# Gate projections of a two-layer streaming encoder: nine seven-product units per layer in place of six of the eight plain gate tiles

## The chip, the cores and the metric

The kernel runs on one core of a Trainium2 chip. The metric is the device time of one execution in microseconds (us): 2654.01 us, the median of three runs (2653.74 to 2655.6). Five engines work beside each other, each with its own queue: TensorE (PE, and PEld for its weight loads), VectorE (DVE), ScalarE (ACT), GpSimd (POOL) and SyncE (SP), which here only issues DMAs.

## The reference

Two layers over 640 tokens (512 of a prompt, 8 x 16 of samples). The mixer in the middle of each layer is what the change touches:

```python
def _layer(h, ...):
    h = h + 0.5 * _rmsnorm(_swiglu(_rmsnorm(h, g[0]), f1g, f1u, f1d), g[1])
    m, ... = _mixer(_rmsnorm(h, g[2]), ...)
    h = h + _rmsnorm(m, g[3])
    return h + 0.5 * _rmsnorm(_swiglu(_rmsnorm(h, g[4]), f2g, f2u, f2d), g[5])

def _mixer(u, ...):
    proj = u @ w_in            # 1024 -> 1792 (pool, q, k, v, conv) + 3 * 1024 gate logits gl
    ...                        # y_pool (256 wide), y_att (512), y_conv (256)
    gates = sigmoid(gl.reshape(bsz, n, 3, 1024) + b_gate)
    merged = (gates[:, :, 0] * (y_pool @ w_branch[:256])
              + gates[:, :, 1] * (y_att @ w_branch[256:768])
              + gates[:, :, 2] * (y_conv @ w_branch[768:]))
    return merged @ w_out
```

All is float32; inputs and outputs too.

## The kernel before

Activations lie transposed: 128 channels on the partitions, tokens along the free axis in two halves `hf` of 320. Every matrix product is made of three passes of 128x128 weights over 320 columns: weight high x activation high, weight high x activation low, weight low x activation high. A weight tile's high part is a rounded copy (`w_hi`, ACT), its low part the difference (`w_lo`, DVE or POOL). Weights come from HBM into four buffers `raw0` to `raw3`, and are staged from there into four slots of `w_hi` and `w_lo`.

The order is written out by hand: each engine has its own program, and semaphores tie them. Per layer it runs the first feed-forward block, the mixer, and the second feed-forward block. The wide products of the feed-forward blocks are already made in units of seven products instead of eight (`strassen`, lines 755 to 757 hold the matmuls): four input blocks (two halves of the contraction, two token halves) and four weight blocks are combined by sums, so that two output tiles for both token halves need 7 x 4 x 3 = 84 matmuls where the plain way needs 8 x 4 x 3 = 96. In such a unit ACT makes the high parts, DVE the sums of weights and the low part of the first slot, POOL five low parts of 128x512.

The mixer's gates are made the plain way. A loop over the eight output tiles `m` (`pe.Fori(0, KD)`) runs, for one tile, `group`s of 24 matmuls for three gates and two token halves, and the three branch products (2, 4 and 2 tiles of contraction, for both halves): 6 x 24 + 2 x 8 x 3 = 192 matmuls. ACT takes the sigmoid (L1621), DVE scales the sums from PSUM (L2115), multiplies with the branch products and adds (`merge`, L2277 to L2281), and ACT and DVE split the merged tile into `mg_hi` and `mg_lo` (L2291). The weights of two slots at a time are a "pair": ACT L1201, then DVE L1761. POOL has nothing in this loop. SP loads a pair as soon as its `raw` buffers are free; after the loop it stores the rows of the pool and conv state (`pc_out`, L606 and L610), and then loads `w_out`. After the gates 16 groups of 24 matmuls multiply by `w_out`, the columns of which are four pairs.

Of the kernel before, what the change touches and what calls it, by code (L numbers as in the profile page):

```python
# [8 lines left out]
F32R = mybir.dt.float32r  # L9
# [46 lines left out]
MIX_PAIRS = MIX_PROJ + 2 * KD + KD // 2  # L56
MIX_GROUPS = 4 * MIX_PROJ + 12 * KD + 2 * KD
# [7 lines left out]
MIX_RAW = [len([p for p in range(MIX_PAIRS) if p % 2 == s // 2]) for s in range(4)]  # L65
# [30 lines left out]
def trunk_kernel(nc, x_prompt, x_sample, state_pool, state_conv, cache_k, cache_v, norm_g, ffn1_w_gate,  # L96
# [5 lines left out]
    with ctx:  # L102
# [22 lines left out]
        mg_lo = view("mg_lo", 2 * RS * HT, at_r, F32R)  # L125
# [37 lines left out]
        mg_hi = view("mg_hi", KD * NT, at_z, F32R)  # L163
# [9 lines left out]
        w_lo = view("w_lo", 4 * WS, at_w + 16 * WS, F32R)  # L173
        at_w23 = (at_w + 8 * WS, at_w + 24 * WS)
# [49 lines left out]
        prod = sem("prod")  # L224
        snap1, snap2, snap3 = sem("snap1"), sem("snap2"), sem("snap3")
# [104 lines left out]
        def mg_op(part, k, hf):  # L330
            return slot_r(mg_lo, hf, 16 + k) if part else tile(mg_hi, k, hf)
# [45 lines left out]

        def raw_full_mix(s, l, p):
            return 16 * LOADS * (l * LAYER_RAW[s] + FFN_RAW[s] + p + 1)
# [4 lines left out]
        def mix_slot(p, s):  # L384
            return 2 + s if p in (1, MIX_PAIRS - 1) else s

# [90 lines left out]
        def _(sp):  # L477
# [92 lines left out]
            for l in range(DEPTH):  # L570
# [3 lines left out]
                def pair(p, parts, at=None, first=None):  # L574

                    for s in range(2):
                        at_p = p if at is None else at
                        slot = 2 * (p % 2) + s
# [19 lines left out]
                with sp.Fori(0, KD) as m:  # L598
                    pm = m * 2 + MIX_PROJ
                    pair(MIX_PROJ, lambda s, slot: columns(w_in, l, 0, KD, m * P + COL_GATE + D * s, slot), pm)  # L600
                    pair(MIX_PROJ + 1, lambda s, slot: branch_rows(l, m, slot) if s else
                         columns(w_in, l, 0, KD, m * P + COL_GATE + 2 * D, slot), pm + 1)

                sp.wait_ge(pc_made, l + 1)
# [7 lines left out]
                for i in range(KD // 2):  # L612
                    pair(MIX_PROJ + 2 * KD + i, lambda s, slot: columns(w_out, l, 0, KD, (2 * i + s) * P, slot))
                last = w0 + MIX_TILES
                head(1, l, [(w_split, last - 1), (w_split, last), (w_split, last - 3), (w_split, last - 2)])
# [22 lines left out]
        def _(pe):  # L638
# [407 lines left out]

            def mixer(l, seam):
# [76 lines left out]
                with pe.Fori(0, KD) as m:  # L1124
                    pm, gm = m * 2 + MIX_PROJ, g + 4 * MIX_PROJ + 12 * m
                    pair_groups(MIX_PROJ, pm, gm, x_op)
# [11 lines left out]
                po, go = MIX_PROJ + 2 * KD, g + 4 * MIX_PROJ + 12 * KD  # L1138
                for q in range(4):
                    if q % 2 == 0:  # L1140
                        pe.wait_ge(mg_ready, 2 * KD * l + 2 * KD - 1 + q // 2)
                    group(tile_of(po, q % 2), q % 2, go + q, q, mg_op, K8, q // 2)
                pair_groups(po + 1, po + 1, go + 4, mg_op)
                for q in range(8):
# [9 lines left out]
                    group(tile_of(p, c % 2), mix_slot(p, c % 2), go + 8 + q, c, mg_op, K8, q // 4, between)  # L1154
# [36 lines left out]
        def _(act):  # L1191
# [340 lines left out]

            def mixer(l, sm):
                g = l * GROUPS + MIX_GROUP0

                def pair_high(p, s, used, at=None):

                    slot = 2 * (p % 2) + s
                    full = raw_full_mix(slot, l, p // 2 if at is None else at)
                    stage(full, mix_slot(p, s), KD, (group_done, used) if used is not None else None, slot)  # L1540
# [83 lines left out]
                def round_merged(m, hf):  # L1624
                    act.wait_ge(merged, 2 * KD * l + 2 * m + hf + 1)
                    alone(act)
                    copy(at_tile(mg_hi, m, hf), xv[hf][:, :]).then_inc(mg_hi_made, 1)

                def merge_tile(m, last):

                    gm, u = g + 4 * MIX_PROJ + 12 * m, 6 * KD * l + 6 * m
# [988 lines left out]
```

## Time and profile before

| what | us |
|---|---|
| median of 3 runs | 2654.01 |
| the profiled execution, its own time | 2655.74 |
| its span, first to last instruction | 2653.9 |
| PE busy in the span | 2632.4 (99%) |
| DVE busy | 1705.1 (64%) |
| ACT busy | 1073.1 (40%) |
| POOL busy | 901.3 (34%) |

Busy time is the time in which an engine executes something. Matmuls overlap: one lasts 309 ns, but the next starts before it has ended, so a PE that is 99% busy is one whose matmuls follow each other almost without a gap. A line is counted where the instruction is issued, often in a helper. In the views by line a row gives the engine, the operation, what it writes and reads, the count, the busy time with the mean of one, and the idle time of the engine just before. "Clock" is the clock that TensorE was granted, 1.00 for its full level.

### The profile page before, as it was taken

The page shows a single profiled execution, that of the slowest core. Times are in us where ns is not written, and L with a number is a line of the kernel's source. Part 1 is how long each engine was busy: PE and PEld are TensorE (multiplying, and loading weights), DVE is VectorE, ACT ScalarE, POOL GpSimd, SP SyncE. Part 2 cuts the span into 40 slices and gives each one's busy share as a digit, 9 for nine tenths or more (in the row PEclk, how much of TensorE's full clock was granted, in tenths as well). Part 3 has the DMA queues.
Part 4 walks back from the last instruction along what each step waited for, and adds up shares of the span by engine and source line. Part 5 has one row for each costly group of instructions (what it writes and reads, how often), then busy time and mean ns, then how long its engine had stood idle before and what let it go on. Part 6 is the DMA issues. An engine that isn't in the chain of part 4 may idle for free.

```text
span 2653.9 us, 52846 instructions
## 1 busy us (share of the span) xinstructions
PE 2632.4 (99%) x17936; PEld 2592.2 (98%) x17936; DVE 1705.1 (64%) x2592; ACT 1073.1 (40%) x1938; POOL 901.3 (34%) x730
## 2 busy tenths in 40 slices
PE   9999999999999999999999999999999999999998
PEld 8999999989999999999999999998999999999998
DVE  7888824664454888882488886266554457988623
ACT  5444513333333544452344444143333344444412
POOL 4655203140001565530256651043100035666112
PEclk9999999999999999999999999999999999999999
DMA  4232323212222222323222232231222222322321
GB/s 131 72 93 81 88 77 90 85 48 73 78 74 82 62 73 81 92 75 87 84 72 80 79 94 85 69 109 54 65 71 71 81 79 58 87 79 87 88 73 62
DMA packets 431022, 210.44 MB, mean 79 GB/s; under 512 B 44777, under 2 KB 429259, under 8 KB 430859
## 3 DMA queue, kind: packets, MB, share of 16 engines
q1 hardware_dynamic: 427252, 205.17, 27.0%
q10 hardware_dynamic: 3638, 3.51, 0.4%
q8 instruction: 84, 1.38, 0.2%
q14 instruction: 48, 0.39, 0.0%
HBM read 205.12 MB, written 5.29 MB: 79 GB/s over the span
## 4 chain that ended last, share of the span: by engine, by line
PE 92%; DVE 6%; ACT 1%; issue 1%; POOL 1%; DVEq 0%; ACTq 0%; POOLq 0%
PE ps L755 11%; PE ps L757 11%; PE ps L756 11%; PE ps L661 9%; PE ps L663 9%; PE ps L662 9%; PE ps L860 7%; PE ps L861 7%; PE ps L862 7%; PE ps L691 5%; PE ps L743 4%; DVE mid_lo L2022 2%; PE ps L1010 1%; PE ps L988 1%; PE ps L891 1%
## 5 line engine op out<-in xcount | busy, mean ns | idle before, releaser
L2447 POOL TENSOR_TENSOR w_lo<-raw,w_hi 128x512 fp32r<-128x512 f32 x288 | 426.5, 1491 | 362.9 <-ACT w_hi L1193 361.2
L755 PE MATMUL ps<-x_r,w_hi 128*128 128x320 f32 x1728 | 534.2, 309 | 0.0
L757 PE MATMUL ps<-x_r,w_lo 128*128 128x320 f32 x1728 | 534.0, 309 | 0.0
L1761 DVE TENSOR_TENSOR w_lo<-raw,w_hi 128x1024 fp32r<-128x1024 f32 (+1 forms) x236 | 289.8, 1232 | 340.7 <-ACT w_hi L1201 340.6
L2398 POOL TENSOR_TENSOR acc_y<-acc_y,sq 128x320 f32<-128x320 f32 x95 | 95.3, 1003 | 1086.8 <-ACT sq L1211 1083.4
L756 PE MATMUL ps<-x_r,w_hi 128*128 128x320 f32 x1440 | 445.0, 309 | 0.0
L1201 ACT ACTIVATE w_hi<-raw 128x1024 fp32r<-128x1024 f32 (+1 forms) x244 | 248.9, 1026 | 470.7 <-PE ps L862 293.9
L860 PE MATMUL ps<-mid_hi,w_hi 128*128 128x320 f32 x1392 | 433.6, 311 | 5.1 <-DVE mid_lo L2022 4.5
L861 PE MATMUL ps<-mid_lo,w_hi 128*128 128x320 f32 x1392 | 430.2, 309 | 0.0
L862 PE MATMUL ps<-mid_hi,w_lo 128*128 128x320 f32 x1392 | 430.1, 309 | 0.0
L661 PE MATMUL ps<-x_r,w_hi 128*128 128x320 f32 x1088 | 345.3, 317 | 0.0
L663 PE MATMUL ps<-x_r,w_lo 128*128 128x320 f32 x1088 | 336.1, 309 | 0.0
L662 PE MATMUL ps<-x_r,w_hi 128*128 128x320 f32 x1088 | 336.0, 309 | 0.0
L1193 ACT ACTIVATE w_hi<-raw 128x512 fp32r<-128x512 f32 (+1 forms) x360 | 255.8, 713 | 176.9 <-DVE raw L1891 87.8
L755 PEld LDWEIGHTS ps<-x_r,w_hi 128*128 128x128 f32 x1728 | 324.4, 188 | 0.8 <-issue 0.8
L757 PEld LDWEIGHTS ps<-x_r,w_lo 128*128 128x128 f32 x1728 | 324.4, 188 | 0.0
L756 PEld LDWEIGHTS ps<-x_r,w_hi 128*128 128x128 f32 x1440 | 270.3, 188 | 0.0
L860 PEld LDWEIGHTS ps<-mid_hi,w_hi 128*128 128x128 f32 x1392 | 261.4, 188 | 7.6 <-DVE mid_lo L2022 7.2
L861 PEld LDWEIGHTS ps<-mid_lo,w_hi 128*128 128x128 f32 x1392 | 261.4, 188 | 0.3
L862 PEld LDWEIGHTS ps<-mid_hi,w_lo 128*128 128x128 f32 x1392 | 261.3, 188 | 0.0
L661 PEld LDWEIGHTS ps<-x_r,w_hi 128*128 128x128 f32 x1088 | 204.2, 188 | 11.2 <-issue 6.2
L662 PEld LDWEIGHTS ps<-x_r,w_hi 128*128 128x128 f32 x1088 | 204.5, 188 | 0.2
(235 smaller groups left out, 5093.0 us busy)
## 6 DMA issues: line engine op xcount, KB each, us to landing
raw<-in_ffn_w_gate_dram SPq DMA_DIRECT2D x352, 128.0 KB, 2.3
raw<-in_ffn_w_up_dram SPq DMA_DIRECT2D x352, 128.0 KB, 2.3
raw<-in_ffn_w_down_dram SPq DMA_DIRECT2D x348, 128.0 KB, 2.2
raw<-in_w_in_dram SPq DMA_DIRECT2D x304, 128.0 KB, 2.3
raw<-in_w_branch_dram SPq DMA_DIRECT2D x64, 128.0 KB, 2.6
raw<-in_w_out_dram SPq DMA_DIRECT2D x64, 128.0 KB, 2.3
raw<-in_ffn_w_down_dram SPq DMA_DIRECT2D x68, 64.0 KB, 1.9
rows<-in_x_prompt_dram SPq DMA_DIRECT2D x4, 512.0 KB, 6.0
```

Of the source, the lines that this page charges most:

```text
L661: pe.matmul(bank(b), wh, op(0, k, hf), start=k == ks[0], stop=False)
L662: pe.matmul(bank(b), wh, op(1, k, hf), start=False, stop=False)
L663: mm = pe.matmul(bank(b), wl, op(0, k, hf), start=False, stop=k == ks[-1])
L755: pe.matmul(bank(b), wh, lhs(0, k), start=begin and k == 0, stop=False, skip_group_check=True)
L756: pe.matmul(bank(b), wh, lhs(1, k), start=False, stop=False, skip_group_check=True)
L757: mm = pe.matmul(bank(b), wl, lhs(0, k), start=False, stop=k == QK - 1, skip_group_check=True)
L860: pe.matmul(bank(b), wh, mid_op(0, k, hf), start=first and k == a, stop=False, skip_group_check=True)
L861: pe.matmul(bank(b), wh, mid_op(1, k, hf), start=False, stop=False, skip_group_check=True)
L862: mm = pe.matmul(bank(b), wl, mid_op(0, k, hf), start=False, stop=last and k == z - 1, skip_group_check=True)
L1193: return act.activation(dst, src, ACT.Copy)
L1761: dve.tensor_tensor(w_cols(1, hi_slot, 0, nk), raw_cols(raw_slot, 0, nk), f32(w_cols(0, hi_slot, 0, nk)), ALU.subtract).then_inc(w_split, 1)
L2447: pool.tensor_tensor(w_cols(1, slot, k0, k0 + QK), src, f32(w_cols(0, slot, k0, k0 + QK)), ALU.subtract).then_inc(ws_lo, 1)
```

## The change

Of the eight output tiles two (`PLAIN_M = 2`) stay as they were; their loop is written out. The other six are made in nine units per layer (`GATE_U = 9`): three pairs of tiles, each for the three branches b = u mod 3. A unit has the seven products P1, P2, P6, P5, P7, P4, P3 of 12 matmuls. The branch products of a unit's two tiles (s = 0 and 1) run in the following unit, the first behind P2 and the second behind P7. Their weights come by DMAs of their own into `br_raw`, which lies in `w_lo` slot 3, so that the low part is made in place. Of the four combinations of activations that the units need, three are made during the two plain tiles (`block_sums`), the fourth (`difference_high`) at the first unit. POOL makes five low parts of 128x512 per unit. The merged tiles are held in `mg` and two other buffers, and split into the slots of `x_r` in the last unit. The first pair of `w_out` takes slots 0 and 1 during the last unit, the second pair slots 2 and 3 behind the last branch product (before: slots 0 and 1 for both, the last pair alone in 2 and 3). The stores of `pc_out` come before the units, and ACT and DVE wait for their end. The diff, cut to its core:

```diff
+PLAIN_M = 2
+GATE_U = 3 * (KD - PLAIN_M) // 2
+BRANCH_K = ((0, 2), (2, 6), (6, 8))
+BRANCH_BANKS = (4, 6, 7)
+        br_raw = view("br_raw", QK * P, at_w + 16 * WS + 4 * (3 * WS + QK * P))
         def mix_slot(p, s):
-            return 2 + s if p in (1, MIX_PAIRS - 1) else s
+            return 2 + s if p in (1, PLAIN_PAIRS + 1, MIX_PAIRS - 1) else s
...
@@ SP @@
+                def gate_unit(u):
+                    for s in range(2):
+                        slot = 2 * ((PLAIN_PAIRS + u) % 2) + s
+                        free = (w_split, w0 + 2 * (PLAIN_PAIRS + u) + s - 3) if u < 2 else (gu_lo, low_gate("B22", l, u - 2))
+                        load(slot, columns(w_in, l, 0, KD, COL_GATE + D * (u % 3) + P * gate_tile(u, s), slot), free)
+                def branch(u, s):
+                    b = u % 3
+                    if u == 0:
+                        sp.wait_ge(gu_prod, prod_gate("P1", l, 0))
+                    elif b == 0:
+                        sp.wait_ge(br_done, 2 * branch_no(l, u - 1, s))
+                    else:
+                        sp.wait_ge(br_done, 2 * (branch_no(l, u, 0) if (b, s) == (1, 1) else branch_no(l, u - 1, 1)))
...
+                for u in range(2):
+                    gate_unit(u)
                 sp.wait_ge(pc_made, l + 1)
...
+                for u in range(GATE_U):
+                    if u + 2 < GATE_U:
+                        gate_unit(u + 2)
+                    else:
+                        out_pair(u + 2 - GATE_U, [(gu_lo, low_gate("B22", l, u))] * 2)
+                    for s in range(2):
+                        branch(u, s)
...
@@ PE @@
+                for u in range(GATE_U):
+                    at, a, d = GATE_U * l + u, BANK_A[u % 2], BANK_D[u % 2]
+                    first = u == 0
+                    pe.wait_ge(gu_w0_lo, at + 1)
...
+                    product("P1", u, lambda part, k: x_op(part, k, 0), a, True)
+                    if not first:
+                        pe.wait_ge(gu_c11_out, at)
+                    product("P2", u, lambda part, k: x_op(part, QK + k, 0), BANK_E, True)
+                    if not first:
+                        branch(u - 1, 0)
+                    pe.wait_ge(gu_lo, low_gate("T2", l, u))
+                    pe.wait_ge(gu_snap1, at + 1)
+                    product("P6", u, lambda part, k: s_op(1, part, k), a, False, made(1) if first else None)
+                    pe.wait_ge(gu_lo, low_gate("T1", l, u))
...
+                    product("P5", u, lambda part, k: s_op(0, part, k), d, True, made(0) if first else None)
+                    pe.wait_ge(gu_lo, low_gate("T3", l, u))
+                    pe.wait_ge(gu_snap2, at + 1)
+                    product("P7", u, lambda part, k: x_op(part, k, 1), a, False, s3_made if first else None)
+                    if not first:
+                        branch(u - 1, 1)
+                    pe.wait_ge(gu_lo, low_gate("T4", l, u))
+                    pe.wait_ge(gu_snap3, at + 1)
+                    product("P4", u, lambda part, k: x_op(part, QK + k, 1), a, False)
+                    pe.wait_ge(gu_lo, low_gate("B22", l, u))
+                    pe.wait_ge(gu_c22_out, at + 1)
+                    product("P3", u, lambda part, k: s_op(2, part, k), d, False, made(2) if first else None)
+                for s in range(2):
+                    branch(GATE_U - 1, s)
-                with pe.Fori(0, KD) as m:
+                for m in range(PLAIN_M):
...
@@ ACT, gates() @@
+                    if first:
+                        for k in range(QK):
+                            difference_high(k)
+                        for what in ("T3", "T4"):
+                            t_high(what, 0, None)
+                        b22_high(0)
+                        snap(u, "P6", u2[u % 2][:, :], a, None, gu_snap2)
...
+                    if final:
+                        merged_high(range(0, 6))
+                    else:
+                        t_high("T2", u + 1, "P6")
+                        t_high("T1", u + 1, "P5")
+                    if u:
+                        branch_high(u - 1, 1)
...
+                act.wait_ge(pc_stored, 16 * PC_STORES * (l + 1))
+                gates(l, g + 4 * MIX_PROJ + 12 * PLAIN_M, difference_high, pair_high)
...
@@ DVE, gates() @@
+                    else:
+                        gate_w0_low(l, u + 1)
+                        gate_sums_second(l, u + 1)
+                    if u:
+                        merges(u - 1, 0)
+                    if final:
+                        merged_low(range(2, 6))
+                    if u:
+                        branch_low(u - 1, 1)
...
@@ DVE, plain tiles @@
+                    block_sums(2 * m)
                     gate(4, u, gm + 4, 0)
-                    merge(0, gm + 5, u + 7)
-                    merged_low(m, 0)
+                    block_sums(2 * m + 1)
+                    merge(m, 0, gm + 5, u + 7)
```

On ACT the loop over tiles alternates sigmoids with the two pairs. One turn of it had, in its second part (`mg_hi` is the merged tile's high part, `xv` the merged tile):

```order
L1193 ISA [waits merged]
L1193 ACTIVATE mg_hi<-xv_122 128x320
L1201 ACTIVATE w_hi<-raw_126 128x1024 [waits group_done,raw_loaded2]
L1619 REGISTER_ALU
L1621 ACTIVATE sig_110<-scaled_112,prm 128x320 [waits evac]
L1200 REGISTER_ALU [waits raw_loaded3]
L1201 ACTIVATE w_hi<-raw_127 128x1024 [waits group_done]
```

Now ACT has this in the third unit (u = 2), from the copy of P1 (`s_0_52<-ps`) to the copy of P7 (`u_56<-ps`); `br_raw` holds the branch weights of the unit before, and `gu_prod` counts the products:

```order
L1385 ACTIVATE s_0_52<-ps 128x320 [waits gu_c11_out,gu_prod]
L1385 ACTIVATE w_hi<-raw_124 128x1024 [waits gu_prod,raw_loaded0]
L1768 ACTIVATE sq_131<-sq_131,prm 128x320 [waits gu_scaled]
L1385 ACTIVATE u_0_54<-ps 128x320 [waits gu_c12_out,gu_prod]
L1385 ACTIVATE w_hi<-raw_124 128x512 [waits gu_prod,gu_t_made]
L1385 ACTIVATE w_hi<-t_one 128x512 [waits gu_prod,gu_t_made]
L1385 ACTIVATE w_hi<-br_raw 128x512 [waits br_in1]
L1385 ACTIVATE u_56<-ps 128x320 [waits gu_c22_out,gu_prod]
```

The high part of the second branch tile stands behind the high part of `t_one` (T1), which waits for P5.

On DVE the same unit has, from the low part of slot 0 to the read of C22 (`tb` are the terms to be added into `mg`):

```order
L2503 TENSOR_TENSOR w_lo<-raw_124,w_hi 128x1024 [waits gu_w0_hi]
L2523 TENSOR_TENSOR raw_124<-t_one,raw_125 128x512 [waits gu_t_made,gu_w0_lo]
L2525 TENSOR_TENSOR raw_124<-raw_124 128x512 [waits gu_t_made]
L2575 TENSOR_TENSOR tb_141<-ps,sq_132 128x320 [waits br_done,merged,gu_sig]
L2575 TENSOR_TENSOR tb_142<-ps,acc_x_137 128x320 [waits br_done]
L2565 TENSOR_TENSOR mg<-mg,tb_141 128x320 [waits br_out]
L2565 TENSOR_TENSOR mg<-mg,tb_142 128x320 [waits br_out]
L2546 TENSOR_TENSOR w_lo<-br_raw,w_hi 128x512 [waits br_hi_made]
L2620 TENSOR_TENSOR diag_133<-ps,u_56 128x320 [waits gu_snap3]
```

The loop before had the scaling, the multiplications and additions with the pairs' low parts between them:

```order
L2277 TENSOR_TENSOR xv_122<-ps,sig_105 128x320 [waits sig_done]
L2274 REGISTER_ALU
L2279 TENSOR_TENSOR tb_142<-ps,sig_107 128x320 [waits group_done]
L2280 REGISTER_ALU
L2281 TENSOR_TENSOR xv_122<-xv_122,tb_142 128x320 [waits evac]
```

The low part of the second branch tile now stands behind four instructions of the merge.

On SP the stores of `pc_out` stood behind the last turn of the loop; now they stand behind the loads of the second unit:

```order
L557 DMA raw_127<-in_w_in_dram 128x2x128 [waits w_split]
...
L557 DMA raw_125<-in_w_in_dram 128x2x128 [waits w_split]
L557 DMA raw_125<-in_w_in_dram 128x2x128 x3
L704 DMA out_dram<-pc_out 15x256 [waits pc_made]
L704 DMA out_dram<-pc_out 2x256
...
L557 DMA raw_126<-in_w_in_dram 128x2x128 [waits gu_lo]
```

The last row is the load of the third unit, behind all stores.

## Rows read from the trace of the kernel before

**Rows 1.** Table by time, columns in its first row: gate loop, then feed-forward units.
```profile
core 0: us, PE busy (x) PEld busy (x) DVE busy (x) ACT busy (x) POOL busy (x), PEclk, DMA share, GB/s
596.50:821.80 225.30, 225.30 (x1538) 225.30 (x1537) 108.95 (x182) 77.79 (x108) 0.00 (x0) 1.00 0.26 74
...
96.00:318.00 222.00, 220.83 (x1504) 220.30 (x1503) 198.38 (x286) 114.23 (x226) 119.03 (x81) 1.00 0.31 87
```

**Rows 2.** The chain that ended last, 600 to 866 us; then whom PE waited for longest.
```profile
by line: PE ps L663 33.4%; PE ps L662 33.4%; PE ps L661 33.3%
...
PE ps L860 <- DVE mid_lo L2022: 4.5, 4, 1.1
```

**Rows 3.** PE by line: count, busy us, mean ns, idle before.
```profile
L755 PE MATMUL ps<-x_r,w_hi 128*128 128x320 f32 x1728 | 534.2, 309 | 0.0
...
L661 PE MATMUL ps<-br_hi,w_hi 128*128 128x320 f32 x256 | 79.1, 309 | 0.0
```

**Rows 4.** ACT by line and shape, same columns.
```profile
L1193 ACT ACTIVATE w_hi<-raw 128x512 fp32r<-128x512 f32 x288 | 179.5, 626 | 125.5 <-DVE raw L1891 87.8 <-PE ps L743 19.9 <-PE ps L757 17.0
L1193 ACT ACTIVATE w_hi<-raw 128x1024 fp32r<-128x1024 f32 x72 | 76.4, 1061 | 51.4 <-PE ps L757 44.7 <-PE ps L743 6.6
...
L1193 ACT ACTIVATE u<-ps 128x320 f32<-128x320 f32 x148 | 64.6, 437 | 260.1 <-PE ps L757 259.2
...
L1193 ACT ACTIVATE br_hi<-ps 128x256 fp32r<-128x256 f32 x20 | 7.7, 385 | 22.0 <-PE ps L1038 13.9 <-PE ps L1043 8.1
```

**Rows 5.** DVE by line and shape.
```profile
L1761 DVE TENSOR_TENSOR w_lo<-raw,w_hi 128x1024 fp32r<-128x1024 f32 x172 | 219.6, 1277 | 143.3 <-ACT w_hi L1201 143.1
L1872 DVE TENSOR_TENSOR w_lo<-raw,w_hi 128x1024 fp32r<-128x1024 f32 x72 | 141.6, 1967 | 33.7 <-ACT w_hi L1193 33.5
...
L1905 DVE TENSOR_TENSOR up<-up,inv_x 128x320 f32<-128x320 f32 x108 | 79.2, 734 | 5.9 <-DVE up L1902 1.2
...
L1882 DVE TENSOR_TENSOR t_one<-raw,raw 128x512 f32<-128x512 f32 x72 | 51.7, 718 | 0.0
...
L2115 DVE TENSOR_TENSOR scaled<-ps,inv_x 128x320 f32<-128x320 f32 x96 | 47.2, 492 | 160.4 <-PE ps L663 160.4
...
L2281 DVE TENSOR_TENSOR xv<-xv,tb 128x320 f32<-128x320 f32 x64 | 31.5, 492 | 2.2
...
L2162 DVE TENSOR_TENSOR br_lo<-ps,br_hi 128x256 fp32r<-128x256 f32 x16 | 6.7, 417 | 6.8 <-ACT br_hi L1193 6.8
```

**Rows 6.** DVE in order of time, a low part made beside POOL in a feed-forward unit.
```profile
205.18 2.32 DVE L1872 TENSOR_TENSOR w_lo<-raw,w_hi 128x1024 fp32r<-128x1024 f32 x1
```

**Rows 7.** POOL by line and shape.
```profile
L2447 POOL TENSOR_TENSOR w_lo<-raw,w_hi 128x512 fp32r<-128x512 f32 x288 | 426.5, 1491 | 362.9 <-ACT w_hi L1193 361.2 <-POOL acc_x L2403 1.4
```

**Rows 8.** DMA issues: count, size of one, median us from issue to landing.
```profile
raw<-in_w_in_dram SPq DMA_DIRECT2D x304, 128.0 KB, 2.3
raw<-in_w_branch_dram SPq DMA_DIRECT2D x64, 128.0 KB, 2.6
...
out_dram<-kv_out SPq DMA_DIRECT2D x32, 8.0 KB, 1.4
```

**Rows 9.** Instructions in order of time on ACT, then DVE, second plain tile: start, us.
```profile
638.97 1.06 ACT L1201 ACTIVATE w_hi<-raw 128x1024 fp32r<-128x1024 f32 x1 [2.01 <-PE ps L663]
...
640.07 1.22 DVE L1761 TENSOR_TENSOR w_lo<-raw,w_hi 128x1024 fp32r<-128x1024 f32 x1 [0.51 <-ACT w_hi L1201]
```

**Rows 10.** SP in order of time, around the second and the last gate tile.
```profile
641.52 2.67 SPq L489 DMA_DIRECT2D raw<-in_w_branch_dram  x4
...
786.00 5.28 SPq L610 DMA_DIRECT2D out_dram<-pc_out  x16
```

**Rows 11.** PE in order of time where its clock fell, and the table by time there.
```profile
908.28 0.41 PE L691 MATMUL ps<-x_r,w_hi 128*128 128x320 f32 x1 [0.53 <-DVE x_r L1779]
909.36 2.81 PE L691 MATMUL ps<-x_r,w_hi 128*128 128x320 f32 x11 [0.66 <-DVE x_r L1779]
...
911.40:914.80 3.40, 3.40 (x13) 3.01 (x12) 2.84 (x5) 3.37 (x5) 0.00 (x0) 0.50 0.11 31
```

More of the change, by code:

```diff
@@ L604, in _, with out_pair @@
+                def out_pair(i, first=None):
+                    pair(PLAIN_PAIRS + i, lambda s, slot: columns(w_out, l, 0, KD, (2 * i + s) * P, slot), first=first)
+                for u in range(2):
+                    gate_unit(u)
                 sp.wait_ge(pc_made, l + 1)
@@ L611, in _ @@
                                       pc_out[DEC_T * (b + 1) - nr:DEC_T * (b + 1), c:c + 2 * P]).then_inc(pc_stored, 16)
-                for i in range(KD // 2):
-                    pair(MIX_PROJ + 2 * KD + i, lambda s, slot: columns(w_out, l, 0, KD, (2 * i + s) * P, slot))
+                for u in range(GATE_U):
[5 more added lines that the diff above has]
+                        branch(u, s)
+                for i in range(2, KD // 2):
+                    out_pair(i)
                 last = w0 + MIX_TILES
-                head(1, l, [(w_split, last - 1), (w_split, last), (w_split, last - 3), (w_split, last - 2)])
+                head(1, l, [(w_split, last - 3), (w_split, last - 2), (w_split, last - 1), (w_split, last)])
                 ffn(1, l)
@@ L1629, in merge_tile, with sums_high @@
-                def merge_tile(m, last):
-                    gm, u = g + 4 * MIX_PROJ + 12 * m, 6 * KD * l + 6 * m
+                    act.activation(x_op(0, k, 1), (acc_x + acc_y)[k][:, :], ACT.Copy, scale=gcol(l, 2, k)).then_inc(gs3_hi, 1)
+                def sums_high(k):
+                    at = QK * l + k
+                    if k:
+                        act.wait_ge(gs_made, 3 * at - 2)
+                    act.activation(sq[0][:, :], tile(h, QK + k, 1), ACT.Copy, scale=gcol(l, 2, QK + k)).then_inc(gs_a22, 1)
+                    for j in range(3):
+                        act.wait_ge(gs_made, 3 * at + j + 1)
+                        copy(s_op(j, 0, k), (sq[1], diag[0], diag[1])[j][:, :]).then_inc(gs_hi, 1)
@@ L1643, in merge_tile @@
[L1643 to L1646 removed]
+                    if m + 1 < PLAIN_M:
+                        pair_high(p + 2, 1, gm + 12)
                 act.wait_ge(kv_stored, 16 * KV_STORES * (l + 1))
                 alone(act)
[L1649 removed]
+                for m in range(PLAIN_M):
+                    merge_tile(m)
+                act.wait_ge(pc_stored, 16 * PC_STORES * (l + 1))
@@ L2331, in mixer @@
                 a = (sm + 1, y_mix, l, 3)
-                pair_low(po + 3, 0)
-                take(0)
-                pair_low(po + 3, 1)
-                for q in range(1, 4):
+                for q in range(4):
                     take(q)
```

462 lines of the change are left out of this document (401 added, 61 removed).

## The prediction, made before the changed kernel ran

> **What bounds the kernel now.** I read the table by time first, over the stretch that the change rewrites: the gate loop of the first layer. In its 225.30 us PE is busy for all 225.30, the clock is at 1.00 (2.4 GHz), DVE is busy for 108.95, ACT for 77.79 and POOL for nothing [rows 1]. The loop issues 8 x 192 = 1536 matmuls, so one costs 225.30 / 1536 = 0.1467 us; its 309 ns [rows 3] are mostly overlap. Next the chain of waits: from 600 to 866 us it consists of the three matmul lines alone, a third each [rows 2]. The view of who waited for whom agrees: PE's longest total anywhere is 4.5 us, in the down projections, and the gate matmuls have no idle time before them [rows 2, 3]. So PE's matmul count sets the time here, nothing is hidden behind another engine, and a matmul less is worth 0.1467 us in full, as long as what feeds PE keeps up. Units of the kind that the change brings exist already in the feed-forward blocks. There DVE is busy for 198.38 of 222.00 us (89%) and POOL for 119.03, and PE still for 220.83 [rows 1], with no idle before L755 [rows 3]. So such units can run without a gap, but with little room on DVE.
>
> **What goes.** A unit makes in 84 matmuls what took 96. Nine units in two layers: 18 x 12 = 216 matmuls, 216 x 0.1467 = 31.7 us. The branch products keep their count (192 per layer), and so does `w_out`. The removed work of DVE and ACT was beside PE: worth nothing. The sums of activations in the two plain tiles are 12 DVE and 16 ACT instructions of about half a us in 56 us in which DVE is half idle, with POOL wholly free for their low parts: nothing.
>
> **Timetable of a unit.** A product is 12 x 0.1467 = 1.76 us. From a matmul's start to the next is 0.147, its end comes 0.16 later, and a waiting engine starts 0.04 after its releaser has ended (ACT ends at 638.97 + 1.06 = 640.03, DVE starts at 640.07 [rows 9]): I take 0.2 us from the end of a product to its reader's start. A unit with the branch products of the one before has 108 matmuls (15.8 us), or 132 (19.4 us) where these are the attention branch's. DVE per unit: 1.97 (low of slot 0, beside POOL) + 4 x 0.72 (sums) + 4 x 0.49 (PSUM reads) + 3 x 0.73 (scaling) + 0.8 to 1.4 (branch lows) + 4 x 0.49 (products with the branches) + up to 4 x 0.49 to 0.73 (additions) [rows 5] = 12 to 15 us. POOL: 5 x 1.49 = 7.5 us [rows 7]. Mean use of DVE is about that of the feed-forward units, so throughput is not the limit; order is. Most things have a unit's length to be ready. Four places don't:
>
> 1. Second branch tile, behind P7. Let e be the end of the first tile's product. P6, P5, P7 give 5.28 us. ACT makes its high part only behind T1's, which waits for P5: e + 3.52 + 0.2 + 0.63 (T1 [rows 4]) = e + 4.35. With two contraction tiles: + 0.39 (ACT, 256 columns [rows 4]) + 0.42 (DVE [rows 5]) = e + 5.16, just in time if nothing stretches it; T1's and T2's low parts run on POOL at that moment, and beside POOL the DVE's 1024-column low part takes 1.97 on average where it takes 1.28 otherwise [rows 5], once 2.32 [rows 6]. Bounds 0 and 1.0 late; I take 0.3, since most stretched ones grow by half: five units per layer, 1.5 us.
> 2. The same with four contraction tiles. Its load waits for the first tile's product (one buffer): e + 0.2, two issues of 0.67 (2.67 / 4 [rows 10]), landing 2.6 after the second's start [rows 8] = e + 3.5, before ACT comes to it. Then e + 4.35 + 0.63 + 0.72 = e + 5.70: 0.4 late, up to 1.4 when stretched; I take 0.7. Units 2 and 5: 1.4 us. In the last unit six high parts of the merged tiles (0.44 each and more) stand ahead in place of T2 and T1, from e + 2.4 to about e + 5.1; then 0.63 + 0.72: e + 6.4, 1.1 us late.
> 3. The last unit's first branch tile: its load waits for the second product of unit 7, and P4 and P3 give 3.52 us: 0.2 + 2.6 + 0.39 + 0.42 = 3.6, with the hand-overs 0.3 us late.
> 4. Entry. P1 is due at 596.5 + 2 x 28.16 = 652.8. ACT's first high part waits for the stores of `pc_out` to end. SP comes to them when the second unit's loads are issued, where the second load row ends now: 641.52 + 2.67 = 644.2, or 0.6 earlier; 18 issues of 5.28 / 16 = 0.33 us end at about 650.1 [rows 10], and 1.4 us (stores of `kv_out` [rows 8]) later the last has landed: 651.5. Then 1.06 (ACT) and 1.28 (DVE): P1 at 653.9, 1.1 us late; without the stores it would be 0.2, with a slower landing 2. What is queued behind ACT's wait are the units' high parts; behind DVE's are the sums and the merge of the last plain tile, whose banks P5 needs only 5 us later. P6 then needs T2's low part: three sums on DVE to 655.9, ACT to 656.6, POOL behind T1's low part 656.9 to 658.4, due at 657.4: 1.0 late (bounds 0.5 and 1.5). The first unit has no branch between P7 and P4, so P4 waits for ACT's copy of P7: 0.2 + 0.44 + 0.05 = 0.7. Entry: 2.8 us.
>
> Sum per layer: 1.5 + 1.4 + 1.1 + 0.3 + 2.8 = 7.1 us; two layers 14.2. Net 31.7 - 14.2 = 17.5 us.
>
> Costed at nothing: the loads of the next units (8 issues from 2.5 us into a unit, landed by 9, read 5 us or more later; behind a held-up branch load they land by 14 and are read at 22); POOL's low parts (a unit of time each); `w_out`'s pairs. The first pair's low parts are made in the last unit. The second pair waits for the last branch product and is due 72 + 24 matmuls (14 us) later, with about 7 us of work on ACT and DVE ahead of it. If that cover were gone it would cost the 1.06 + 1.28 of one slot. The last merged tiles (k = 6, 7) are read 10.6 us behind the branch products and need about 6. The way from the mixer into the next block keeps its instructions.
>
> **A rule against the change.** On what the low parts cost beside POOL the rows give growth by half on average, 0.69 on 1.28 [rows 5]. The Trainium skill (SBUF — State Buffer, Who interferes with whom) says that a DVE instruction with two SBUF inputs and a GpSimd instruction that reads SBUF hold the shared read interface in turn, whichever issues second being fully blocked until the first ends. The trace agrees in kind: PSUM-reading L2115 stays at 492 ns, and the 2.32 us one has 1.04 more than the mean alone. By the mean growth the sum is the one above; by a full block at each place it is the second rival.
>
> **The rivals.** *Everything covered*: the feed-forward units carry as much and have no gap [rows 1, 3]; against it stand the entry's fixed chain and place 2. With only 1.5 us left per layer, net 28.7: 2627 in the profiled execution, 2625 as a median; with less than that 2622.
>
> *A full block at each branch tile*: the second tile's low part has to wait for the whole of T1's low part on POOL (1.49 us [rows 7]): 5.16 + 1.49 - 5.28 = 1.4 late in five units, 0.4 + 1.49 = 1.9 in two. 7.0 + 3.8 + 1.1 + 0.3 + 2.8 = 15.0 per layer, net gain 1.7: 2652, no change.
>
> *Slower: the clock falls at these stalls.* At 908 to 910 us two waits of 0.53 and 0.66 us for DVE come close together, and then from 911.40 to 914.80 the clock stands at 0.50 (1.2 GHz), and 13 matmuls start in 3.40 us, which at 0.1467 each would be 1.9 [rows 11]: 1.5 us lost. If the blocked branch tiles brought this in eight units of a layer, that would be 15.0 + 12.0 = 27.0 per layer, 54 - 31.7 = 22 us slower: 2677 (2675 as a median). It decides from a mean of 31.7 / 18 = 1.8 us lost per unit. Against it: PE also waited in the down projections, up to 1.1 us at once [rows 2], and the clock table of the whole stretch 96 to 318 stays at 1.00 [rows 1]; and these waits would be 16 us apart, one at a time.
>
> That fewer matmuls are issued but each costs more is not plausible, since both kinds of group show 309 ns without idle [rows 3].
>
> **How the numbers follow.** The profiled execution before took 2655.74 us, its span 2653.9, and the median is 1.7 below it. 2655.74 - 17.5 = 2638.2; as a median 2636.5. Chances: forecast 0.55 (its own range 2628 to 2647), everything covered 0.26, full block 0.13, slower 0.06. 0.2% is 5.3 us and about what a measurement tells here. Faster by more: 0.55 + 0.26 + half of the block case, less a little for the forecast's tail: 0.86. Within: 0.07; slower: 0.07. The range for 8 in 10 reaches from the covered case to just short of the block case: 2622 to 2650.
>
> **What would show it.** PE's count falls by 216 to 17720. PE idle stands before the first matmul of P6, P4 and P1 in the first unit, and before L1177 (first matmul of a branch tile) behind P7, released by DVE's L2546; little stands before all other products. L2546 has two durations, short where POOL is idle. The clock in the gate stretch stays 1.00. I am wrong on the size of the stalls if PE waits elsewhere, above all before P1 or P3 of units 1 to 7 (DVE behind altogether), or if the matmul pitch in the units is not 0.147 us; and on the entry if ACT doesn't wait for the stores.

## The result and the profile after

| | median of 4 runs, us | lowest to highest | span of the profiled run |
|---|---|---|---|
| before | 2653.88 | 2653.3 to 2655.6 | 2653.9 |
| after | 2668.07 | 2666.92 to 2668.7 | 2666.5 |

The ratio is 1.0052 (95% interval 1.004 to 1.0064): the changed kernel is 14 us slower, where 17.5 us faster was forecast. The forecast was wrong in its sign, and the result lies outside its range of 2622 to 2650.

First the page after, its first lines and the chain:

```profile
span 2666.5 us, 51480 instructions
...
PE 2611.7 (98%) x17720; PEld 2564.3 (96%) x17720; DVE 1823.4 (68%) x2756; ACT 1130.4 (42%) x2114; POOL 1057.7 (40%) x860
...
PE 87%; DVE 9%; ACT 2%; issue 2%; POOL 1%; DMA 0%; DVEq 0%; SPq 0%; ACTq 0%; POOLq 0%
```

PE's count is the forecast one, and still PE holds only 87% of the chain (92% before). Next whom PE waited for (total us, times, longest), the answer to the waits of [rows 2]:

```profile
PE ps L1177 <- DVE w_lo L2546: 16.0, 16, 2.1
PE ps L1161 <- ACT u L1385: 9.8, 2, 4.9
PE ps L965 <- DVE mid_lo L2346: 4.9, 7, 1.1
...
PE ps L1177 <- DVE tb L2575: 2.4, 2, 1.4
...
PE ps L1161 <- DVE w_lo L2503: 1.9, 2, 1.0
PE ps L1161 <- POOL w_lo L2987: 1.7, 2, 0.9
...
PE ps L1161 <- DVE x_r L2589: 1.4, 2, 0.7
```

All but the third are new. L1177 is the first matmul of a branch product, L1161 that of a unit's own products. The same by time, from the last matmul that reads `wp_now`, among the last projections, to the first of the layer's next sum (it reads `ones`): first and second layer after, then before. Columns as in [rows 1].

```profile
592.37:872.94 280.57, 263.77 (x1758) 259.81 (x1756) 183.47 (x287) 120.36 (x217) 88.21 (x73) 0.99 0.27 76
1904.94:2185.82 280.88, 264.43 (x1757) 260.49 (x1755) 183.44 (x287) 120.33 (x217) 88.15 (x73) 0.98 0.27 76
```
```profile
592.75:866.37 273.62, 273.62 (x1865) 273.32 (x1864) 126.40 (x205) 91.67 (x129) 13.60 (x12) 1.00 0.27 78
```

Before, PE is busy for all of it; after, it is idle for 16.80 and 16.45 us, and the clock is below 1.00. The account, from the starts of PE's matmuls:

- Before, the stretch has 1864 matmuls and took 273.62 us, 0.17 above 1864 x 0.1467.
- After, it has 1756 and took 280.57 and 280.88 us, which is 22.96 and 23.28 above 1756 x 0.1467. So a layer saved 108 x 0.1467 = 15.84 us and lost 23.1.
- Between the two stretches it is 1032.00 us in both kernels. From the second to the last matmul it is 473.43 us after and 474.68 before: the clock fell there at 2215 us before, and not after. Ahead of the first it is 592.37 after and 592.75 before.
- Sum: 6.95 + 7.26 - 1.25 - 0.38 = 12.6, the difference of the spans.

Where the 22.96 us of the first layer went (each matmul's start less the one before, less 0.147). The second layer repeats every wait within 0.03 us but the last, which is 1.15: there the clock had stood at half from 2129.2 to 2132.6 us, for 1.5 us more.

| place | at, us | forecast | measured |
|---|---|---|---|
| entry, P1 | 653.6 | 1.1 | 1.12 |
| entry, P6 | 658.3 | 1.0 | 1.04 |
| entry, P7, two waits | 662.0, 663.4 | 0 | 1.06 |
| entry, P4 | 670.0 | 0.7 | 5.05 |
| clock at half behind it | 668.3 to 675.1 | 0 | 2.3 |
| second branch tiles of units 0 to 6, seven waits of 0.83, 1.10 or 1.16 | 687 to 796 | 2.9 | 7.0 |
| last unit, second branch tile | 816.1 | 1.1 | 2.27 |
| last unit, last branch product | 827.4 | (0.3, another place) | 1.53 |
| second matmul behind each wait, about 0.1 longer | | 0 | 1.6 (the rest) |

**The 5 us wait.** PE, ACT, DVE and POOL of the changed kernel in order of time, unit 0 ending and unit 1 beginning (start us, duration, ..., idle before and its releaser):

```profile
664.76 0.31 PE L1163 MATMUL ps<-x_r,w_lo 128*128 128x320 f32 x1
669.95 0.60 PE L1161 MATMUL ps<-x_r,w_hi 128*128 128x320 f32 x1 [4.89 <-ACT u L1385]
670.36 0.47 PE L1162 MATMUL ps<-x_r,w_hi 128*128 128x320 f32 x1
```
```profile
660.64 1.05 ACT L1385 ACTIVATE w_hi<-raw 128x1024 fp32r<-128x1024 f32 x1
666.56 0.56 ACT L1768 ACTIVATE sq<-sq,prm 128x320 f32<-128x320 f32 x1 [4.87 <-DVE sq L2534]
668.34 0.63 ACT L1385 ACTIVATE w_hi<-raw 128x512 fp32r<-128x512 f32 x1 [1.21 <-DVE raw L2523]
668.87 0.61 ACT L1385 ACTIVATE w_hi<-t_one 128x512 fp32r<-128x512 f32 x1
669.39 0.42 ACT L1385 ACTIVATE u<-ps 128x320 f32<-128x320 f32 x1
```
```profile
660.32 3.07 DVE L2589 SCALAR_TENSOR_TENSOR x_r<-acc_x,prm,x_r 128x320 fp32r<-128x320 f32 x2
663.31 1.00 DVE L2589 SCALAR_TENSOR_TENSOR x_r<-acc_y,prm,x_r 128x320 fp32r<-128x320 f32 x2
664.23 0.68 DVE L2513 TENSOR_TENSOR t_one<-raw,raw 128x512 f32<-128x512 f32 x1
...
665.44 0.48 DVE L2603 TENSOR_TENSOR sq<-ps,s 128x320 f32<-128x320 f32 x1
...
667.61 0.69 DVE L2523 TENSOR_TENSOR raw<-t_one,raw 128x512 f32<-128x512 f32 x1
```
```profile
658.74 4.29 POOL L2987 TENSOR_TENSOR w_lo<-raw,w_hi 128x512 fp32r<-128x512 f32 x3 [0.55 <-ACT w_hi L1385]
```

P4 reuses the bank of P7, so it waits for ACT's copy of P7 (`u<-ps`), possible since about 665.1 (its last matmul starts at 664.76). On ACT that copy is queued behind the sigmoid of C11 (C11, C12, C21 and C22 are a unit's four results, which DVE reads from PSUM) and the high parts of T2 and T1 of unit 1; these wait for DVE, and DVE comes late to C11 and to the sums, because four low parts of S3, the fourth combination of activations, stand ahead: beside POOL two take 3.07 us, with POOL idle two take 1.00. PE stands still for one copy of 0.42 us, while ACT and POOL are idle for most of the time and DVE makes what is due later. P7's two waits are for the first two of these four. Then the clock: P4's and P3's matmuls start 0.267 us apart from 670.36 to 675.13, at 1.2 GHz, where 0.147 was due.

**The second branch tile.** The changed kernel in unit 1, ACT, DVE, POOL, PE:

```profile
684.91 0.63 ACT L1385 ACTIVATE w_hi<-t_one 128x512 fp32r<-128x512 f32 x1 [0.86 <-PE ps L1163]
685.45 0.40 ACT L1385 ACTIVATE w_hi<-br_raw 128x256 fp32r<-128x256 f32 x1
```
```profile
685.88 1.30 DVE L2546 TENSOR_TENSOR w_lo<-br_raw,w_hi 128x256 fp32r<-128x256 f32 x1 [1.68 <-ACT w_hi L1385]
```
```profile
685.62 1.28 POOL L2987 TENSOR_TENSOR w_lo<-t_one,w_hi 128x512 fp32r<-128x512 f32 x1 [0.19 <-ACT w_hi L1385]
```
```profile
687.25 0.41 PE L1177 MATMUL ps<-br_hi,w_hi 128*128 128x320 f32 x1 [0.67 <-DVE w_lo L2546]
```

ACT's high part of T1 releases POOL, ACT's next instruction releases DVE 0.26 us later, and the 256-column low part, 0.42 us of work [rows 5], takes 1.30. It ends at 687.18, 0.28 us behind POOL's. So do all twenty 256-column low parts that came 0.26 to 0.31 us behind POOL's start, whatever POOL took (1.3 to 1.5 us); the ten of 512 columns end 0.55 behind it. The other six met no POOL instruction and took 0.42 (256 columns) and 0.69 (512). Over the run (DVE by line and shape):

```profile
L2546 DVE TENSOR_TENSOR w_lo<-br_raw,w_hi 128x256 fp32r<-128x256 f32 x24 | 29.8, 1240 | 12.1 <-ACT w_hi L1385 12.0
...
L2546 DVE TENSOR_TENSOR w_lo<-br_raw,w_hi 128x512 fp32r<-128x512 f32 x12 | 15.7, 1309 | 12.4 <-ACT w_hi L1385 12.4
...
L2575 DVE TENSOR_TENSOR tb<-ps,acc_x 128x320 f32<-128x320 f32 x24 | 11.6, 484 | 2.7 <-PE ps L1179 2.5
```

The mean of 1240 ns mixes twenty low parts of 1.30 to 1.49 us with four of 0.42. The instruction that reads PSUM keeps its 0.48 us; the six of its kind that lie wholly beside a POOL instruction took 0.49.

### The profile page after: what moved, and what is told of

The parts are those of the page before. It is cut to its first block, busy times and chain, and to the rows that moved or that the text cites. A ratio compares the mean times of both kernels' runs of the same rounds, so it can differ in the third digit from the quotient of the medians.

```text
span 2666.5 us, 51480 instructions
## 1 busy us (share of the span) xinstructions
PE 2611.7 (98%) x17720; PEld 2564.3 (96%) x17720; DVE 1823.4 (68%) x2756; ACT 1130.4 (42%) x2114; POOL 1057.7 (40%) x860
## 4 chain that ended last, share of the span: by engine, by line
PE 87%; DVE 9%; ACT 2%; issue 2%; POOL 1%; DMA 0%; DVEq 0%; SPq 0%; ACTq 0%; POOLq 0%
PE ps L860 11%; PE ps L861 11%; PE ps L862 11%; PE ps L965 7%; PE ps L967 7%; PE ps L966 7%; PE ps L796 5%; PE ps L848 4%; PE ps L766 4%; PE ps L768 4%; PE ps L767 4%; DVE mid_lo L2346 2%; PE ps L1161 2%; PE ps L1163 2%; PE ps L1162 2%
## 5 line engine op out<-in xcount | busy, mean ns | idle before, releaser
L860 PE MATMUL ps<-x_r,w_hi 128*128 128x320 f32 x1728 | 534.3, 309 | 0.0
L862 PE MATMUL ps<-x_r,w_lo 128*128 128x320 f32 x1728 | 533.9, 309 | 0.0
L2085 DVE TENSOR_TENSOR w_lo<-raw,w_hi 128x1024 fp32r<-128x1024 f32 (+1 forms) x188 | 231.6, 1238 | 319.0 <-ACT w_hi L1393 318.8
L861 PE MATMUL ps<-x_r,w_hi 128*128 128x320 f32 x1440 | 444.9, 309 | 0.0
L1385 ACT ACTIVATE w_hi<-raw 128x512 fp32r<-128x512 f32 (+1 forms) x450 | 319.7, 713 | 244.3 <-DVE raw L2215 87.2
L1393 ACT ACTIVATE w_hi<-raw 128x1024 fp32r<-128x1024 f32 (+1 forms) x196 | 198.0, 1017 | 362.8 <-PE ps L967 293.9
L860 PEld LDWEIGHTS ps<-x_r,w_hi 128*128 128x128 f32 x1728 | 324.3, 188 | 0.8 <-issue 0.8
L861 PEld LDWEIGHTS ps<-x_r,w_hi 128*128 128x128 f32 x1440 | 270.3, 188 | 0.0
L766 PE MATMUL ps<-x_r,w_hi 128*128 128x320 f32 x704 | 227.3, 323 | 0.0
L768 PE MATMUL ps<-x_r,w_lo 128*128 128x320 f32 x704 | 217.5, 309 | 0.0
L767 PE MATMUL ps<-x_r,w_hi 128*128 128x320 f32 x704 | 217.4, 309 | 0.0
L1385 ACT ACTIVATE u<-ps 128x320 f32<-128x320 f32 x184 | 80.3, 437 | 309.1 <-PE ps L862 259.4
L861 PE MATMUL ps<-sp_r,w_hi 128*128 128x320 f32 x576 | 178.0, 309 | 0.0
```

The costliest lines, as they stand in the source:

```text
L766: pe.matmul(bank(b), wh, op(0, k, hf), start=k == ks[0], stop=False)
L767: pe.matmul(bank(b), wh, op(1, k, hf), start=False, stop=False)
L768: mm = pe.matmul(bank(b), wl, op(0, k, hf), start=False, stop=k == ks[-1])
L860: pe.matmul(bank(b), wh, lhs(0, k), start=begin and k == 0, stop=False, skip_group_check=True)
L861: pe.matmul(bank(b), wh, lhs(1, k), start=False, stop=False, skip_group_check=True)
L862: mm = pe.matmul(bank(b), wl, lhs(0, k), start=False, stop=k == QK - 1, skip_group_check=True)
```

## The experiments

All are the changed kernel with the edits shown, each run 5 to 11 times; the medians of the kernel before beside them were 2653.59 to 2653.88. Traces, waits and excess are those of one run of each. "Excess" is the time of a layer's stretch above 0.1467 us per matmul, 22.96 and 23.28 in the changed kernel.

**ACT's copy of P7 first.**

```
+ if first: snap(u, "P7", ...)        # ahead of C11's sigmoid, T2, T1 highs of unit 1
  sigmoid(u, "C11", ...)
  ...
- snap(u, "P7", ...)                  # now only for u > 0
```

> Only ScalarE's order in the first unit of each layer is changed: its copy of P7 stands ahead of the C11 sigmoid and of T2's and T1's high parts of the second unit. Theory A (the 5.05 us wait before P4 is ScalarE's order alone, and the clock fall behind it follows from it): the wait shrinks to 0.7 us and the clock stays at 1.00, 4.35 + 2.3 us per layer, 13.3 in all: 2668.07 - 13.3 = 2654.8. Theory B (VectorE is itself late, with four S3 low parts and the second unit's sums ahead of its read of C22): P4 starts in time, but P3 then waits for VectorE until about 669.6 us, 2.3 us; the gain is 2.0 us per layer and the clock fall may go or stay: 2659 to 2664.

Measured 2664.56 (2660.16 to 2667.8), ratio 1.0038 (1.0025 to 1.0052). PE in order of time:

```profile
666.52 0.38 PE L1161 MATMUL ps<-x_r,w_hi 128*128 128x320 f32 x1 [0.62 <-ACT u L1385]
670.36 0.38 PE L1161 MATMUL ps<-sp_r,w_hi 128*128 128x320 f32 x1 [1.86 <-issue]
```

P4 starts after 0.6 us, and the clock stays at 2.4 GHz in the first unit of the traced run. But P3 now waits 2 us, as theory B had it, though the median lies 0.6 us above its range: DVE reads C22 only at 669.78, behind unit 1's low part and four sums. The copy was the last cause, not the only one. The excess is 19.2 in both layers. In this run the clock fell in both last units instead (813 and 2120 us), behind their 2.27 us wait. The five runs are 7.6 us apart: the two near 2660 have a mean clock of 0.998, the two near 2667 one of 0.995. The traced run is one of the fast ones (2660.27), so where the clock fell in the others isn't known.

**Also DVE's read of C22 first.**

```
+ if u == 0: take22()                 # DVE: C22 = bank + u, its scaling
  gate_w0_low(l, u + 1); sums of T2, T1
+ if u: take22()
```

> As the run before, and VectorE reads C22 of the first unit ahead of the second unit's slot-0 low part and sums. Theory A: no difference from the run before (2654.8). Theory B: the wait that moved to P3 goes, PE waits 0.7 us before P4 and under 0.3 before P3, no clock fall in the first unit: 2654 to 2656, so 5 to 9 us less than the run before.

Measured 2661.75 (2661.24 to 2662.58), 1.0028 (1.0017 to 1.0038): a miss. The wait of P3 is gone, and a new one stands behind P1 and P2 of the next unit, before its first branch tile:

```profile
674.80 0.42 PE L1177 MATMUL ps<-br_hi,w_hi 128*128 128x320 f32 x1 [1.39 <-DVE w_lo L2549]
```

ACT makes that branch tile's high part at 673.25, behind five others, the first of which waited 2.14 us for DVE's sum. The second branch tile of that unit waits 1.23 us. Excess 19.64 and 18.19; in the first layer, where the clock fell at the same places as in the run before, it is 0.4 more. So this edit moved the wait and gained nothing of it.

**Was it the load?** On top of the last edit, SyncE issues the first unit's branch weights ahead of the third unit's gate weights.

```
+ for s in range(2): branch(0, s)
  for u in range(GATE_U): gate_unit(u + 2) ...
```

> As e7_entry_both (2661.75), and SyncE loads the first unit's branch weights ahead of the third unit's gate weights. Theory (what is late in the second unit now, 1.55 us before the first branch tile, is that load queued behind eight others which wait for GpSimd's last low part of the first unit): this wait goes and the second tile's falls back from 1.24 to 0.84; about 1.9 us per layer, 2658. Rival (VectorE is late there because it was put behind C22): both stay, 2661.7.

Measured 2662.43 (2661.62 to 2662.71), 1.0031 (1.0018 to 1.0043), with both waits as before (1.54 and 1.24): it was not the load. That it was ACT's queue a later run shows (ACT's high part of the first unit's first branch tile earlier).

**ACT's high part of the second branch tile earlier** (ahead of T2's, for attention between T2's and T1's; the copy and C22 stand as in the changed kernel, and the expectation compares with the run that comes next here):

```
+ if u and not final and (u - 1) % 3 != 1: branch_high(u - 1, 1)
  t_high("T2", u + 1, "P6")
+ if u and (u - 1) % 3 == 1: branch_high(u - 1, 1)
  t_high("T1", u + 1, "P5")
```

> As e3_both_early, but only ScalarE's high part of the second branch tile stands earlier; VectorE keeps its order (merge first). Theory (the place on VectorE decides where the merge has additions, the place on ScalarE where it has none): waits go for the pool branch (merge without additions), stay between 0.3 and 1.0 for the conv branch, and fall to 0.4 for the attention branch: 2657 to 2662. Rival (ScalarE's order alone was the cause): as e3_both_early, 2654.5.

Measured 2660.25 (2658.18 to 2662.6), 1.0023 (1.0014 to 1.0033). The time is in the range, the waits not all: five of the seven go, those of the attention branch too, and the two of the conv branch stay at 1.16, where 0.3 to 1.0 was expected. There DVE is still in the merge of the first tile, as in the changed kernel, where this merge runs from 721.45 to 723.4 and the low part comes right behind it. Then **the same with DVE's low part ahead of that merge**:

```
+ if early: branch_low(u - 1, 1)
  merges(u - 1, 0)
- branch_low(u - 1, 1)
```

> The second branch tile's high part (ScalarE) stands ahead of T2's and T1's for two-tile branches and between them for the four-tile one; its low part (VectorE) ahead of the merge for two-tile ones. Theory (the waits of 0.83 to 1.16 us behind P7 are the low part standing on VectorE at the moment of T1's low part on GpSimd, and the order in front of it): five waits per layer go to 0, the two of the four-tile branch from 1.10 to at most 0.4, the last unit's 2.27 stays: 4.9 + 1.4 = 6.3 us per layer, 12.6 in all: 2655.5. Rival (the weights' load is what comes last): unchanged waits, 2668. Rival (the work moved forward is only repaid by later waits at P4, P3 or P1): fewer waits behind P7, new ones elsewhere, 2665 or more.

Measured 2654.5 (2653.19 to 2655.39), 0.9999 (0.999 to 1.0008), 13.6 below the changed kernel by two moved calls. Waits and the low part's duration (a mean of the first tiles', still 1.43 beside POOL, and the second tiles', now 0.42):

```profile
PE ps L1177 <- DVE w_lo L2550: 4.2, 2, 2.1
```
```profile
L2550 DVE TENSOR_TENSOR w_lo<-br_raw,w_hi 128x256 fp32r<-128x256 f32 x24 | 20.2, 843 | 6.2 <-ACT w_hi L1385 6.0
```

Only the last unit's two are left of sixteen. Excess 14.1 in both layers, so 9 us per layer came back. In the first layer these are the seven waits (7.0), the slower matmul behind each (0.7), 0.4 at the last branch product, and 0.8 behind P4, where the clock fell 1 us earlier in the same wait.

**The contention by itself.** POOL's low parts of T2 and T1 for units 1 to 8 cover 32 of 512 columns; the rest of these low parts is left out.

```
- pool.tensor_tensor(w_cols(1, slot, ...), src, ...)
+ n = 32 if u and what in ("T2", "T1") else QK * P
+ pool.tensor_tensor(w_cols(1, slot, ...)[:, 0:n], src[:, 0:n], ...)
```

> GpSimd makes T2's and T1's low parts of units 1 to 8 over 32 of their 512 columns only (the rest of those low parts is left out), everything stands where it stood. Theory (contention for the shared read interface): the 256-column low parts on VectorE fall from about 1.3 to 0.42 us without a change of order, the five waits of 0.83 to 1.16 go to at most 0.2, the four-tile ones to 0.4 to 0.6: 5.5 us per layer, 2657. Rival (order alone, ScalarE's high parts come too late): low parts get shorter, but PE's waits stay above 0.6: 2663 or more.

Measured 2656.31 (2655.4 to 2658.0), 1.0007 (0.9998 to 1.0016); no instruction changed its order.

```profile
PE ps L1177 <- DVE w_lo L2546: 5.3, 6, 2.1
```
```profile
L2546 DVE TENSOR_TENSOR w_lo<-br_raw,w_hi 128x256 fp32r<-128x256 f32 x24 | 20.2, 843 | 15.0 <-ACT w_hi L1385 14.7
```

The five two-tile waits go and attention's fall from 1.1 to 0.4. The second tiles' low parts take 0.42 us in the places where they took 1.30 to 1.49, and the first tiles', whose POOL neighbours were left whole, still 1.43. So by itself the order of the code costs under 0.1 us in a two-tile unit and 0.4 in an attention unit; the rest of each wait was POOL's 1.3 us in the same moment.

**The last unit.** The branch high part after two of the six merged high parts, its low part ahead of four merged low parts (not in the lines below), and the layer's last branch product in bank 5:

```
- merged_high(range(0, 6)); branch_high(u - 1, 1)
+ merged_high(range(0, 2)); branch_high(u - 1, 1); merged_high(range(2, 6))
- b = BRANCH_BANKS[r % 3]
+ b = BANK_E if r == 4 * GATE_U - 1 else BRANCH_BANKS[r % 3]
```

> Changed in the last unit only: the branch tile's high part stands behind two of the six merged high parts instead of six, its low part ahead of four merged low parts, and the layer's last branch product goes to PSUM bank 5, which is free, so that it needn't wait for VectorE to have read the one three before. Theory: the 2.27 us wait falls to 0.5 or less, the 1.53 us wait before the last product (released by VectorE's L2575) goes; the clock fall in the second layer's last unit (3.4 us at half, 1.5 us) goes: 3.3 us per layer and 1.5, 8 in all: 2660. Rival (the last load, which waits for unit 7's second product, is what is late): the second wait stays or moves ahead of the first branch product, 2664.

Measured 2663.25 (2661.96 to 2663.95), 1.0033 (1.0021 to 1.0046). The time is 3 us above the expected 2660, but both waits did what was expected: 2.27 became 0.66 and the 1.53 is gone. So the last branch tile had waited for DVE to read the bank of three products before, not for its load. The clock did not fall in the last units, but at both seams behind them (the way from the mixer into the next block, 915 and 2222 us), as it does before the change [rows 11]. The changed kernel had no fall at the second seam, and behind the second stretch this run took 1.3 us more: this ate some of the gain.

**All of these together**, then with ACT's high part of unit 0's first branch tile right behind its copy of P7, then also with ACT's high part for P1 of unit 0 ahead of the last plain tile's sigmoid and not behind the stores of `pc_out`:

```
+ branch_high(0, 0)                                          # second of the three
+ copy(w_cols(0, 0, 0, KD), raw_cols(r, 0, KD))              # third: in the last plain tile
  gate(l, m, 5, u, gm + 8)
```

> All order changes together: entry (ScalarE, VectorE, SyncE), branch tiles, last unit. If the 216 matmuls are worth 31.7 us and the waits are independent, what is left per layer is the entry's 1.12 + 1.03 + 0.2 + 0.9 + 0.8 and at most 0.5 at the end, 4.5 us, and no clock fall: 2653.9 - 31.7 + 9 = 2631. Rival (waits only move to other products once these go): 2640 or more.

Measured 2639.73 (2639.57 to 2639.89), 0.9946 (0.9932 to 0.9959), excess 7.4: a miss, since 2631 was expected. Of the 6.5 us between the expected span (2631.2) and this one (2637.7), 5.9 lie in the two stretches, where 4.5 per layer was expected. The 1.5 us wait before the first branch tile of the second unit stayed, and the slower matmul behind each wait had no term.

> As e8_all (2639.73), and ScalarE makes the high part of the first unit's first branch tile directly behind its copy of P7, instead of behind five high parts and three sigmoids. Theory (the 1.53 us wait left in the second unit is ScalarE's queue, not the load, which had landed 10 us before): the wait goes, 1.5 us per layer, 2636.7. Rival (VectorE is what is late there): unchanged, 2639.7.

Measured 2637.3 (2636.5 to 2638.88), 0.9935 (0.9921 to 0.9949), as expected. The 1.53 us wait became 0.31, so that one was ACT's queue; 0.6 and 0.3 appeared behind it. Excess 7.05 and 6.81.

> As e11_first_branch, and ScalarE makes slot 0's high part for the first unit ahead of the last plain sigmoid, without waiting for the state's stores. Theory (P1's wait of 1.1 us is the chain sigmoid, high part, low part behind a merge that the sums of activations delay; the stores had landed before): 0.5 us less per layer before P1, and up to as much before P6, whose sums stand behind the same low part: 2635. Rival (P6's wait takes back what P1 gains, and the sum stays): as e11.

Measured **2633.64** (2631.04 to 2634.3), **0.9918** (0.9905 to 0.9932): 20 us faster than the kernel before and 34 faster than the changed one. Its waits:

```profile
PE ps L968 <- DVE mid_lo L2364: 4.7, 6, 1.1
...
PE ps L1164 <- ACT u L1390: 2.2, 4, 0.6
...
PE ps L1164 <- DVE x_r L2608: 2.0, 4, 0.7
...
PE ps L1182 <- DVE w_lo L2564: 1.3, 4, 0.5
...
PE ps L1164 <- POOL w_lo L3015: 0.7, 2, 0.4
```

P1 no longer waits, and P6 waits half as long, as expected. Excess 5.22 and 5.36: with the same matmuls, the order of ACT's, DVE's and SyncE's queues, and one product in another bank, carried 18 of the 23 us per layer.

## Why the prediction was wrong

**Right.** 17720 matmuls, 0.1467 us each, 31.7 us saved in full. P1 (1.12 for 1.1) and P6 (1.04 for 1.0). P3 and P1 of units 1 to 7 have no wait: DVE keeps up over a unit, and the feed-forward units were a fair model for throughput. In the steady units the waits stand before the second branch tiles, as forecast, and L2546 is their releaser. The sign "the clock in the gate stretch stays 1.00" failed (0.99 and 0.98).

**The step that failed: the term for P4, "0.2 + 0.44 + 0.05 = 0.7".** It measured 5.05, and 2.3 more by the clock. The step took ACT as free when P7 ends, and listed nothing of what stands ahead of the copy in ACT's program: an instruction that waits for DVE, whose own queue was long. The four low parts of the fourth combination (4.0 us from 660.32 to 664.31) had no term in the entry at all, though their high parts were known to be made there; they are also P7's two waits. For P6 I had walked through such a chain, engine by engine; for P4 not. The first two experiments show that two queues held P4 and P3, and that the wait then moved to the third reader (the branch tile, 1.55 us) instead of going.

**Places 1 and 2: 2.9 forecast, 7.0 measured.** The choice was "most stretched ones grow by half". The mean in [rows 5] mixes low parts that lie beside POOL for different shares of their time; these meet it every time. In two-tile units of the pool branch and in attention's, two high parts that ACT ends 0.3 to 0.5 us apart release POOL and then DVE; in conv units DVE comes from the merge 0.3 us behind POOL's start. 0.42 became 1.3 to 1.5, and 0.69 became 1.36. The rival of the full block had the mechanism, with 10.8 us for these places; it charged the whole of POOL's 1.49 on top, though POOL had begun a little before and some slack was left. The experiments that moved the low part and that shortened POOL's agree (2654.5 and 2656.3). The Trainium skill (SBUF — State Buffer, Who interferes with whom) calls the ports that the two engines share an exclusive lock. This trace agrees: 1.30 us for 0.42 of work and an end 0.28 us behind POOL's each time, while L2575 stays at 484 ns. The row that the prediction gave for the second half of this, L2115 at 492 ns, could not show it, since it is from the gate loop, in which POOL ran nothing [rows 1].

**The last unit: 2.27 for 1.1, and 1.53 for 0.3.** Six merged high parts ended at 813.1 as worked out, but DVE had four low parts and the merge ahead of the branch's (815.35). I had followed ACT's queue alone. Place 3 did not come: PE has no wait before the first branch tile behind the last unit (823.23). The 1.53 us stand three products later and are for a PSUM bank, for which the timetable had no line.

**P1's reason.** The time was right by luck. ACT made the high part at 651.24, and was not waiting for the stores but for its sigmoid at 650.77, which waited for DVE. That is the prediction's own sign of being wrong on the entry. When the high part was put ahead of that, the wait went. I did not separate the two conditions, since both were taken away in one edit.

**The rival of the clock** gave 2677 and was wrong on the place: the clock did not fall at the branch tiles, whose waits of 0.8 to 1.2 us, 16 to 20 us apart, brought none. It fell in the 5 us wait of each layer (6.8 us at half) and behind the second layer's 2.27 us wait (2129.2 to 2132.6), not the first's. The forecast had all this at nothing; it cost 2.3 us in the first layer and 3.1 in the second. That the measured 2668 lies between the full block's 2652 and this rival's 2675 is no merit of either, since most of it is from P4, which neither had.

By the forecast's own terms, 7.1 in the first layer became 23.0. Of the 15.9 more, 4.3 + 2.3 are P4 and its clock, 4.1 the branch tiles, 2.4 the last unit, 1.1 P7, and 1.6 the slower matmuls behind waits.

## What to carry to other kernels

When a change removes work from the bounding engine, list for each buffer or bank that it waits for the whole queue of the engine that frees it, each queued instruction with its own releaser, at every place where a pattern starts and ends: the steady units cost 7 us per layer here, the first and last 14. Put the instruction that frees the bounding engine ahead of those that only prepare the next unit. And don't let two instructions that follow each other release GpSimd and then VectorE onto SBUF when VectorE's result is due first.

## What the runs showed of the hardware

- In the changed kernel a 128x256 subtraction of two SBUF tensors on DVE took 0.42 us with POOL idle. Starting 0.26 to 0.31 us behind a 128x512 one on POOL it took 1.30 to 1.49, and ended 0.28 to 0.29 us behind POOL's, twenty times out of twenty. Where DVE had started 0.3 us ahead of POOL (ACT's high part earlier) it took 0.42. Two 128x320 operations with two SBUF tensors took 3.07 us beside POOL and 1.00 alone; those with one PSUM input took 0.48 to 0.49 in both cases.
- The first matmul behind a wait is followed 0.22 to 0.25 us later by the next, not 0.147, so each wait costs about 0.1 us more than its length.
- In the traces of the five kernels with the 5.05 us wait the granted clock went to half during it, in both layers, stood there for 6.8 us and came back by itself; in the six without it, it did not fall there. Behind the 2.27 us waits it fell for 3.4 us at eight of fourteen: in both layers of one kernel (ACT's high part earlier) and in neither of another (DVE's low part too). Whether the seam behind a mixer had a fall changed from trace to trace as well: both before, the first alone after, neither where only ACT's copy was moved. Why is open.
